# Cumulative log decays summed once in the projections and read back per chunk, in a chunkwise hybrid recurrence

## The chip, the cores and the metric

The kernel runs on one core of one Trainium2 chip. The metric is the device time of one execution in microseconds (us). All tensors are float32; matmuls whose operands are of type fp32r take one pass over their columns, those of plain float32 operands several, and the trace shows each of the latter as two records.

## What is computed

One layer of a hybrid encoder trunk on 2048 tokens of width 1024: an RMSNorm, one wide input projection, three token mixers, gates, an output projection and a final norm. The change touches the third mixer, a gated DeltaNet in chunkwise form (8 value heads, 4 key heads of 128). Cut to what matters:

```python
log_a = -jnp.exp(a_log) * softplus(c_a + dt_bias)      # one number per token and head
g = jnp.cumsum(log_a, axis=-1)                          # within a chunk
diff = g[..., :, None] - g[..., None, :]
decay_causal = masked_exp(diff, causal)
m = einsum('tk,sk->ts', k, kb) * decay_strict           # kb = k * beta
sol = triangular_solve(I + m, [v, k * exp(g)])
a_qk = einsum('tk,sk->ts', q, kb) * decay_causal
q_inter = q * exp(g);  k_state = kb * exp(g_last - g)
# per chunk: e = u - w S;  o = q_inter S + a_qk e;  S = exp(g_last) S + k_state^T e
```

The kernel uses chunks of 128 tokens (it calls them windows, 16 of them), which gives the same result as the 64 of the reference. The second mixer, HGRN2, runs beside it in the same windows, with its own decays in seven levels.

## The kernel before

Four blocks follow one another, each with its own instruction lists for PE, ACT, DVE, POOL and the DMA-issuing SP, tied by semaphores: `norm_and_transpose` (to about 80 us), `project` (to about 1625 us), `recur` (to about 2275 us) and `merge`. Each engine runs its list in the order in which it is written, so the order of work is the order of the calls in these lists.

`project` makes 80 pairs of output tiles, with seven block products each of 12 fp32r matmuls of 512 columns. `decays_begun` and `decays_ended` (L1229, L1236) leave the log decays and betas of all 2048 tokens in `keep["ab"]`. `fill_masks` (L110) writes the masks on POOL after its last operand.

`recur` works on windows w, with v = w + 1 prepared while w is finished. What the change and the prediction speak of:

- Log decays. `log_decays` (L1486) spreads one window's log decays over a causal mask on POOL, in a high and a low fp32r part (`la_t`). `decays_between` on PE (L1592) multiplies them with `later_r` into the banks `M[0]`, `M[1]`, which gives g_t - g_s in every place, and `decays_from_start` (L1599) with `ones_r` into `M[2]`, `M[3]`, which gives g_t. ACT turns the first into `dec` (L1868) and the second into `eg` (L1874). POOL multiplies `dec` with the betas (`weighted_decays`, L1499), DVE multiplies the products of keys with keys and queries by it (`an_keys` L2054, `an_queries` L2059), and POOL makes the decayed queries from `eg` (L1519).
- Triangular inverse. `blocks_out` (L1416) sends `ak` to DRAM and reads its 16x16 diagonal blocks back as `X`; DVE inverts them (`substitute`); `inverses_back` (L1423) brings them into `T` and `R`. PE and DVE then double the inverse three times: `level_w` and `level_z` with l = 4, 5, 6 on PE (L1692, L1712; L1692, L1709; L1690, L1706), `level_32`, `level_64` and `level_128` on DVE (L2126 to L2144).
- HGRN2. `scores(w, l)` on PE (L1663 to L1669) reads `kql`, which DVE makes in `pair_kq` (L2093) and `level_kq` (L2108).
- End of a window. `products_e`, `products_o`, `products_ds` (L1720 to L1749), the norms of the outputs, and `norms(v + 1)` on PE (L1585), which ACT reads in `key_norms` (L1858, L1860) before `hx_inv` (L1882), the operand of DVE's next `pair_kq`.

The PE list of a window (L1804 on) is: `turn_v`, `products_ks`, `level_w` 4, `turn_k`, `turn_hv`, `decays_between(v)`, `level_z` 4, `products_kq(v)`, `scores` 0, `decays_from_start(v)`, `level_w` 5, `scores` 1, `level_z` 5, `scores` 2, `level_w` 6, `scores` 3, `level_z` 6, `scores` 4, `products_e` and the rest. In windows 1 to 14 the two decay calls stand in this list; those for v = 0 and 1 stand ahead of the loop.

## Time and profile before

| | us |
|---|---|
| median of 3 runs | 2839.93 |
| lowest, highest | 2833.96, 2846.58 |
| the profiled execution | 2831.88 |
| its span, first to last instruction | 2830.1 |
| mean granted TensorE clock | 0.984 of full |
| busy: PE, DVE, ACT, POOL | 2731.2, 1848.6, 1239.0, 1473.3 |

The profile gives for each engine the time in which an instruction of it ran, and for TensorE also the clock that was granted (1.00 is 2.4 GHz, 0.50 is 1.2 GHz). A timeline row has its start, its length (of all instructions merged in it), engine, line, output and inputs, and in brackets how long the engine was idle before it and who ended that.

### The profile page before, as it was taken

Reading aid. Unit: us, or ns where it says so; the run is one execution under the profiler, and the core shown is the slowest. Engines: PE = TensorE matmul, PEld = TensorE weight load, DVE = VectorE, ACT = ScalarE, POOL = GpSimd, SP = SyncE. Lnnn points to the kernel's source line nnn. Section 1 sums busy time; section 2 is a strip of 40 time slices with the busy share of each in tenths; the row PEclk is TensorE's granted clock in tenths of the full one; section 3 lists DMA queues with packets and bytes.
Section 4 is the critical chain, followed back from the end, with each engine's and each line's share of the span. In section 5 each row is a group of like instructions: output and inputs, shape, how many; then the busy total and the mean of one; then the engine's idle time right before and its main releaser. Section 6 shows DMA issues by size and latency. Waiting matters only on the chain. (4 is left out here: it accounts for less than half of the span.)

```text
span 2830.1 us, 39377 instructions
## 1 busy us (share of the span) xinstructions
PE 2731.2 (97%) x14135; PEld 2286.3 (81%) x14135; DVE 1848.6 (65%) x2902; ACT 1239.0 (44%) x2153; POOL 1473.3 (52%) x1135
## 2 busy tenths in 40 slices
PE   7999999999998999999999979999999979999999
PEld 5788888888877888888888768888888867888877
DVE  7777777773248788878722258888888765445453
ACT  7443444444453444444444435566555543222221
POOL 0554555554446555555554466666777435453441
PEclk9999999999999999999999979999999989999999
DMA  6333333334463333333343356665555557555552
GB/s 188 97 112 104 91 112 104 99 95 120 111 183 94 112 90 105 108 106 92 104 119 97 107 129 155 155 154 132 130 134 149 136 180 234 162 182 172 171 174 76
DMA packets 536937, 366.05 MB, mean 129 GB/s; under 512 B 65462, under 2 KB 469032, under 8 KB 536744
## 3 DMA queue, kind: packets, MB, share of 16 engines
q1 hardware_dynamic: 536744, 363.52, 45.2%
q8 instruction: 115, 1.88, 0.3%
q14 instruction: 78, 0.64, 0.1%
HBM read 251.27 MB, written 112.20 MB: 128 GB/s over the span
## 5 line engine op out<-in xcount | busy, mean ns | idle before, releaser
L767 POOL TENSOR_TENSOR w_low<-w_raw,w_high 128x512 fp32r<-128x512 f32 x479 | 684.9, 1435 | 634.8 <-ACT w_high L846 634.7
L800 PE MATMUL p_x<-h_high,w_high 128*128 128x512 f32 x1280 | 500.3, 391 | 13.1 <-ACT u L975 6.5
L800 PE MATMUL p_x<-h_low,w_high 128*128 128x512 f32 x1280 | 499.3, 390 | 0.0
L800 PE MATMUL p_x<-h_high,w_low 128*128 128x512 f32 x1280 | 499.2, 390 | 0.0
L846 ACT ACTIVATE w_high<-w_raw 128x512 fp32r<-128x512 f32 x479 | 296.5, 627 | 246.8 <-PE p_z L800 141.3
L800 PEld LDWEIGHTS p_x<-h_high,w_high 128*128 128x128 f32 x1280 | 240.8, 188 | 66.2 <-ACT u L975 7.3
L800 PEld LDWEIGHTS p_x<-h_low,w_high 128*128 128x128 f32 x1280 | 240.9, 188 | 50.2
L800 PEld LDWEIGHTS p_x<-h_high,w_low 128*128 128x128 f32 x1280 | 241.0, 188 | 49.8
L800 PE MATMUL p_z<-h_high,w_high 128*128 128x512 f32 x640 | 249.2, 389 | 0.0
L800 PE MATMUL p_z<-h_low,w_high 128*128 128x512 f32 x640 | 249.1, 389 | 0.0
L800 PE MATMUL p_z<-h_high,w_low 128*128 128x512 f32 x640 | 249.1, 389 | 0.0
L2442 PE MATMUL b_o<-m_yh,m_wo_high 128*128 128x512 f32 x512 | 202.0, 394 | 21.9 <-DVE m_yl_lead L2578 12.5
L2403 POOL TENSOR_TENSOR m_wo_low<-m_wo_raw_lead,m_wo_high 128x512 fp32r<-128x512 f32 x86 | 118.8, 1384 | 180.4 <-ACT m_wo_high L2497 180.3
L1098 DVE TENSOR_TENSOR c_raw<-p_z,u 128x512 f32<-128x512 f32 x72 | 49.8, 691 | 241.6 <-PE p_x L800 181.3
L2442 PE MATMUL b_o<-m_yh,m_wo_low 128*128 128x512 f32 x512 | 201.0, 393 | 0.0
L767 POOL TENSOR_TENSOR w_low<-w_s,w_high 128x512 fp32r<-128x512 f32 x80 | 114.8, 1435 | 97.9 <-ACT w_high L846 97.3
L1510 POOL TENSOR_TENSOR dx<-hin 128x256 f32<-128x256 f32 x112 | 76.4, 682 | 132.4 <-ACT hx L1893 118.4
L1114 DVE SCALAR_TENSOR_TENSOR ring<-c_raw,cols,ring 128x512 f32<-128x512 f32 x128 | 142.3, 1112 | 4.5
L2541 DVE TENSOR_TENSOR w_raw<-b_o,ring 128x512 f32<-128x512 f32 x96 | 65.8, 690 | 121.2 <-PE b_o L2442 97.0
L800 PEld LDWEIGHTS p_z<-h_high,w_high 128*128 128x128 f32 x640 | 120.2, 188 | 25.2 <-DVE c_raw L1098 0.2
L800 PEld LDWEIGHTS p_z<-h_low,w_high 128*128 128x128 f32 x640 | 120.1, 188 | 25.0
L800 PEld LDWEIGHTS p_z<-h_high,w_low 128*128 128x128 f32 x640 | 120.1, 188 | 24.9
(300 smaller groups left out, 6096.6 us busy)
## 6 DMA issues: line engine op xcount, KB each, us to landing
w_raw<-in_w_in_dram SPq DMA_DIRECT2D x160, 512.0 KB, 5.2
branch_scratch<-ring SPq DMA_DIRECT2D x176, 256.0 KB, 5.2
gate_scratch<-ring SPq DMA_DIRECT2D x96, 256.0 KB, 6.0
ring<-gate_scratch SPq DMA_DIRECT2D x96, 256.0 KB, 4.0
hin<-branch_scratch SPq DMA_DIRECT2D x16, 1280.0 KB, 11.6
zin<-branch_scratch SPq DMA_DIRECT2D x16, 1024.0 KB, 7.0
m_wo_raw_lead<-in_w_out_c_dram SPq DMA_DIRECT2D x43, 256.0 KB, 3.1
xin<-in_x_dram SPq DMA_DIRECT2D x16, 512.0 KB, 3.9
```

The costliest lines, as they stand in the source:

```text
L767: nc.gpsimd.tensor_tensor(wl(j), place(p, j), wh(j).bitcast(F32), ALU.subtract).then_inc(low, 1)
L800: x = nc.tensor.matmul(to[:], w(j)[:, k, :], h[:, j, k, :], start=(opens and k == 0 and a == 0), stop=(k == HK - 1 and a == 2), skip_group ...
L846: fn(wh(j), place(p, j), ACT.Copy).then_inc(high, 1)
L1098: tt(of_unit(p, 1, 1), Z[p % 2][:], u3[:], ALU.add).then_inc(c22, 1)
L1114: link(stt(out, src, w, out, ALU.mult, ALU.add))
L1510: tt(free_ap(dx[:, l % 2, :], 0, halves), left, mid, ALU.subtract)
L2403: tt(wl[:, u % SLOTS, :, :], wraw(u), raw(wh[:, u % SLOTS, :, :]), ALU.subtract).then_inc(w_low, 1)
L2442: x = nc.tensor.matmul(bank, w[:, u % SLOTS, k, :], y(4 * i + k), start=(i < 3 and k == 0 and a == 0), stop=(i != 2 and k == 3 and a == 2))
L2541: tt(to, bank, gt[:, b, :], ALU.mult).then_inc(gated, 1)
```

## The change

The sums g of the log decays are formed once, in `project`. At pair 8 PE multiplies the log decays of all windows with four 128x128 masks (causal, after, ones, and a causal mask less its middle column, "centred"); ACT copies the four results out, PE transposes two of them (sums from the start and centred sums) so that a window's head is a row, ACT copies these too, and SP stores both forms in DRAM. The causal mask is filled at pair 3 instead of at the end, and DVE makes the other two at pair 6.

In `recur` SP loads, for each window, one row of 1024 numbers into all 128 partitions, once of the centred sums (`rows_centred`) and once of the sums from the start (`rows_start`). POOL subtracts the centred sum of the row's own token (`col[:, 3, v, :]`) and cuts the difference at 0 (`exponents`), in place of `log_decays`; ACT takes exponentials of these in place, and of `rows_start` in one instruction. PE's `decays_between` and `decays_from_start` are gone, with the waits that kept their banks apart. Both loads stand behind `blocks_out` in SP's list.

```diff
@@ project: SP @@
+                    if p == 12:
+                        sp.wait_ge(rows_kept, 1)
+                        sp.dma_start(front["decay_rows"].rearrange("i r n -> r i n"), kept_rows).then_inc(decays_out, 16)
+                        sp.dma_start(front["decay_sums"], t3_flat[:, 0:4 * P]).then_inc(decays_out, 16)
@@ project: PE @@
+                def decay_sums_of():
+                    pe.wait_ge(causal_cut, 1)
+                    pe.wait_ge(sum_masks, 2)
+                    for i, which in enumerate((causal[:], after, keep["ones"][:], centred)):
+                        x = nc.tensor.matmul(sums_bank[:, i, :], which, ab[:, :, 0:dm.vh], start=True, stop=True)
+                    x.then_inc(decay_sums, 1)
+                def decay_rows_of():
+                    pe.wait_ge(sums_kept, 1)
+                    for i, at in enumerate((0, 3)):
+                        x = nc.tensor.transpose(rows_bank[:, i, :], kept_sums[:, at, :], keep["ident"][:])
...
@@ project: ACT @@
+                    if p == 9:
+                        act.wait_ge(decay_sums, 1)
+                        fn(kept_sums, sums_bank[:], ACT.Copy).then_inc(sums_kept, 1)
+                    if p == 11:
+                        act.wait_ge(decay_rows, 1)
+                        fn(kept_rows, rows_bank[:, 0:2, :], ACT.Copy).then_inc(rows_kept, 1)
@@ recur: SP @@
+                def load_centred(v):
+                    wait(sp, v - 1, "diff_ready", 1)
+                    sp.dma_start(rows_centred[:].rearrange("p h n -> p (h n)"), bass.AP(rows.tensor, (win + v) * V * P, [[0, P], [1, V * P]])
+                                 ).then_inc(centred_in, 16)
+                def load_start(v):
+                    wait(sp, v - 1, "eg_ready", 1)
...
+                sp.dma_start(col[:].rearrange("p i w c -> p (i w c)"), front["decay_sums"]).then_inc(col_in, 16)
+                load_centred(0)
+                load_start(0)
                 load(0)
...
                 load_k(1)
+                load_centred(1)
+                load_start(1)
                 blocks_out(0)
                 load(1)
                 inverses_back(0)
+                load_centred(2)
...
                         blocks_out(w + 1)
+                        if w + 2 < win:
+                            load_start(w + 2)
+                        if w + 3 < win:
+                            load_centred(w + 3)
                         inverses_back(w + 1)
@@ recur: POOL @@
-                def log_decays(v):
-                    wait(pool, v - 1, "m_ga", 2)
-                    for i in range(2):
-                        tt(la_t[:, i, :, :], free_ap(masks["causal"][:], 0, [[0, V], [1, P]]), spread(la_parts[:, i, v, :].bitcast(F32), P),
-                           ALU.mult).then_inc(sems["la_ready"], 1)
+                def exponents(v):
+                    pool.wait_ge(centred_in, 16 * v + 16)
...
+                    wait(pool, v - 1, "aq_ready", 2)
+                    tt(dec[:], rows_centred[:], spread(col[:, 3, v, :], P), ALU.subtract).then_inc(sems["diff_ready"], 1)
+                    wait(pool, v, "diff_ready", 1)
+                    nc.gpsimd.tensor_scalar(dec[:], dec[:], 0.0, None, ALU.min).then_inc(sems["diff_ready"], 1)
@@ recur: PE, in the loop @@
-                    if 0 < w < win - 1:
-                        decays_between(v)
                     level_z(w, 4)
...
-                    if 0 < w < win - 1:
-                        decays_from_start(v)
                     level_w(w, 5)
@@ recur: ACT @@
+                    wait(act, v, "diff_ready", 2)
                     for g in range(2):
-                        wait(act, v, "m_gb", g + 1)
-                        fn(four(dec, g), M[g][:], ACT.Exp).then_inc(sems["dec_ready"], 1)
+                        fn(four(dec, g), four(dec, g), ACT.Exp).then_inc(sems["dec_ready"], 1)
...
-                    for g in range(2):
-                        wait(act, v, "m_ga", g + 1)
-                        fn(four(eg, g), M[2 + g][:], ACT.Exp).then_inc(sems["eg_ready"], 1)
+                    act.wait_ge(start_in, 16 * v + 16)
+                    fn(eg[:], rows_start[:], ACT.Exp).then_inc(sems["eg_ready"], 1)
```

DVE's list inside the loop is the same in both kernels. On PE, from `level_w` 4 to `products_e` of a window, the list was this (`b_m`, `b_g`, `b_h` are the banks M, G and HB):

```order
L1692 MATMUL b_g<-T,ak 128x64 x8
L1639 MATMUL b_m<-ident,qkn 128x128 x4
L1645 MATMUL b_m<-ident,hin 128x128 x4
L1589 MATMUL b_m<-la_t,later_r 128x512 x4
L1712 MATMUL b_g<-W,R 128x64 x8
L1612 MATMUL b_m<-qkn 128x256 x4
L1663 MATMUL b_h<-kql 128x128 x4
L1589 MATMUL b_m<-la_t,ones_r 128x512 x4
L1692 MATMUL b_g<-T,ak 128x64 x8
L1669 MATMUL b_h<-kql 128x64 x4
L1709 MATMUL b_g<-R,W 64x64 x8
```

In the changed kernel the same stretch reads:

```order
L1732 MATMUL b_g<-T,ak 128x64 x8
L1679 MATMUL b_m<-ident,qkn 128x128 x4
L1685 MATMUL b_m<-ident,hin 128x128 x4
L1752 MATMUL b_g<-W,R 128x64 x8
L1654 MATMUL b_m<-qkn 128x256 x4
L1703 MATMUL b_h<-kql 128x128 x4
L1732 MATMUL b_g<-T,ak 128x64 x8
L1709 MATMUL b_h<-kql 128x64 x4
L1749 MATMUL b_g<-R,W 64x64 x8
```

The two groups of four 512-column matmuls are gone and nothing stands in their place. SP's list in a window of the changed kernel, from the store of the outputs to the inverse blocks, is:

```order
L1467 DMA y_scratch<-ring 128x8x128
L1471 DMA an_scratch<-ak 128x8x128
L1474 DMA X<-an_scratch 64x16x16
L1447 DMA rows_start<-decay_rows_scratch 128x1024
L1442 DMA rows_centred<-decay_rows_scratch 128x1024
L1483 DMA inverse_scratch<-XI 64x16x16
L1485 DMA inverse_scratch<-XT 64x16x16
```

The two loads of 128x1024 are new; the instructions around them are those of before, in their order.

## Rows read from the trace of the kernel before

**Rows 1.** The page, busy time of each engine.

```profile
PE 2731.2 (97%) x14135; PEld 2286.3 (81%) x14135; DVE 1848.6 (65%) x2902; ACT 1239.0 (44%) x2153; POOL 1473.3 (52%) x1135
```

**Rows 2.** Stretches: length, busy PE, PEld, DVE, ACT, POOL, clock, DMA share, GB/s.

```profile
1780.20:1817.90 37.70, 37.07 (x297) 32.91 (x295) 31.87 (x91) 22.57 (x44) 26.70 (x24) 1.00 0.58 145
...
1912.00:1922.00 10.00, 9.36 (x93) 8.82 (x91) 9.18 (x34) 4.14 (x8) 10.00 (x10) 1.00 0.08 8
```

**Rows 3.** Timeline of PE, from one window's `norms` to the next one's.

```profile
1893.49 1.88 PE L1585 MATMUL b_m<-w_raw,ones 128*128 128x512 f32 x4
...
1901.20 1.21 PE L1589 MATMUL b_m<-la_t,later_r 128*128 128x512 f32 x4
1902.24 1.89 PE L1712 MATMUL b_g<-W,R 128*128 128x64 f32 x16
...
1906.57 1.17 PE L1589 MATMUL b_m<-la_t,ones_r 128*128 128x512 f32 x4
1907.57 1.89 PE L1692 MATMUL b_g<-T,ak 128*128 128x64 f32 x16
...
1913.68 0.68 PE L1690 MATMUL b_g<-T,ak 128*64 128x64 f32 x8 [0.60 <-DVE T L2139]
...
1931.18 1.02 PE L1585 MATMUL b_m<-w_raw,ones 128*128 128x512 f32 x2
```

**Rows 4.** Timeline of ACT in that window, from `key_norms` to `hx_inv`.

```profile
1894.62 0.69 ACT L1858 ACTIVATE rn<-b_m,eps 128x512 f32<-128x512 f32 x1 [0.54 <-PE b_m L1585]
...
1897.11 0.61 ACT L1882 ACTIVATE hx_inv<-dx 128x512 f32<-128x512 f32 x1
```

**Rows 5.** Timeline of DVE in that window.

```profile
1897.85 0.69 DVE L2093 TENSOR_TENSOR kql<-hin,hx_inv 128x512 f32<-128x512 f32 x1 [2.24 <-ACT hx_inv L1882]
...
1906.92 1.13 DVE L2108 TENSOR_TENSOR kql<-hin,hx 128x512 f32<-128x512 f32 x1
...
1913.31 0.31 DVE L2139 STREAM_TRANSPOSE T<-b_g 32x128 f32<-32x128 f32 x1
```

**Rows 6.** Waits of PE, 1700 to 2235 us: who, total, times, longest.

```profile
PE b_g L1690 <- DVE T L2139: 8.4, 14, 0.6
PE b_g L1720 <- DVE R L2144: 1.2, 3, 0.6
```

**Rows 7.** Three windows' `products_e` on PE, a stretch, and two of DVE's window starts.

```profile
1765.03 3.64 PE L1720 MATMUL b_g<-w_raw,R 128*128 128x128 f32 x16 [0.61 <-DVE R L2144]
...
1955.61 2.05 PE L1720 MATMUL b_g<-w_raw,R 128*128 128x128 f32 x16 [0.32 <-DVE R L2144]
...
1993.83 3.68 PE L1720 MATMUL b_g<-w_raw,R 128*128 128x128 f32 x16 [0.31 <-DVE R L2144]
...
1994.00:1997.20 3.20, 3.20 (x16) 3.20 (x17) 2.75 (x10) 0.62 (x2) 3.20 (x3) 0.50 0.01 3
...
1744.64 0.69 DVE L2093 TENSOR_TENSOR kql<-hin,hx_inv 128x512 f32<-128x512 f32 x1 [2.31 <-ACT hx_inv L1882]
...
1784.79 0.69 DVE L2093 TENSOR_TENSOR kql<-hin,hx_inv 128x512 f32<-128x512 f32 x1 [2.23 <-ACT hx_inv L1882]
```

**Rows 8.** Window 0: two stretches, and two rows of PE's timeline.

```profile
1670.00:1674.00 4.00, 4.00 (x21) 4.00 (x20) 1.14 (x2) 0.38 (x1) 0.00 (x0) 0.50 0.00 0
...
1690.00:1694.00 4.00, 4.00 (x39) 3.88 (x38) 2.29 (x10) 1.38 (x3) 3.00 (x5) 0.99 0.02 6
...
1657.78 2.06 PE L1589 MATMUL b_m<-la_t,ones_r 128*128 128x512 f32 x4
...
1685.96 1.97 PE L1669 MATMUL b_h<-kql 128*128 128x64 f32 x8
```

**Rows 9.** Two groups of POOL instructions, and a load with its KB and time to landing.

```profile
L1489 POOL TENSOR_TENSOR la_t<-causal,la_parts 128x1024 fp32r<-128x1024 f32 x32 | 60.1, 1898 | 7.2 <-DVE la_parts L2189 7.2
L1499 POOL TENSOR_TENSOR dec<-dec,db 128x1024 f32<-128x1024 f32 x16 | 38.0, 2377 | 50.5 <-ACT dec L1868 50.5
...
w_raw<-in_final_norm_w_dram SPq DMA_DIRECT2D x1, 512.0 KB, 5.7
```

More of the change, by code:

```diff
@@ L597, in project @@
         X, Y, Z = ([bank(f"p_{n}{i}") for i in range(2)] for n in "xyz")
+        sums_bank, rows_bank = (c.enter_context(nc.psum_tensor(f"p_sums{i}", [P, 4, P], F32)) for i in range(2))
+        causal = keep["masks"]["causal"]
+        ab = keep["ab"][:, 0:dm.win * 2 * dm.vh].rearrange("p (w c) -> p w c", c=2 * dm.vh)
         own_sems = []
@@ L632, in project @@
         t2 = craw[:, 0, :, 3:3 + 2 * BLK]
+        t3_flat = t3[:].rearrange("p a n -> p (a n)")
+        kept_sums, kept_rows = (t3_flat[:, at:at + n * P].rearrange("p (i n) -> p i n", n=P) for at, n in ((0, 4), (4 * P, 2)))
+        centred, after = t3_flat[:, 6 * P:7 * P], t3_flat[:, 7 * P:8 * P]
         form_place = {P1: wide(work[:]), P5: wide(work[:]), P2: wide(lows_of(P5)), P6: t2, P4: wide(ring[:]), P3: wide(lows_of(P3))}
@@ L1256, in _ @@
                         decays_ended()
+                    if p == 6:
+                        dve.wait_ge(causal_cut, 1)
+                        tt(centred, causal[:], spread(causal[:, P // 2 - 1:P // 2], P), ALU.subtract).then_inc(sum_masks, 1)
+                        tt(after, keep["ones"][:], causal[:], ALU.subtract).then_inc(sum_masks, 1)
                     q, more = before(p), p + 1 < N
@@ L1571, in _ @@
                 mm, turn, ident = nc.tensor.matmul, nc.tensor.transpose, keep["ident"][:]
-                def columns():
-                    for i, which in enumerate((masks["causal"][:], later_r[:].bitcast(F32), keep["ones"][:])):
-                        x = mm(G[0][:, i, :], which, ab[:, :, 0:V], start=True, stop=True)
-                    x.then_inc(m_col, 1)
                 def norms(v):
@@ L1585, in norms @@
                         mm(M[g][:], keep["ones"][:], sq[:, g, :], start=True, stop=True).then_inc(sems["m_ssq"], 1)
-                def sum_parts(bank, which, g):
-                    for i in range(2):
-                        x = mm(bank[:], which[:], four(la_t[:, i, :, :], g), start=(i == 0), stop=(i == 1))
-                    return x
-                def decays_between(v):
-                    wait(pe, v, "la_ready", 2)
-                    wait(pe, v, "rn_ready", 3)
-                    for g in range(2):
-                        wait(pe, v - 1, "res", 4 * g + 4)
-                        sum_parts(M[g], later_r, g).then_inc(sems["m_gb"], 1)
-                def decays_from_start(v):
-                    if v > 0:
-                        wait(pe, v - 1, "hv_ready", 1)
-                        wait(pe, v - 1, "kt_ready", 1)
-                    for g in range(2):
-                        sum_parts(M[2 + g], ones_r, g).then_inc(sems["m_ga"], 1)
                 def products_kq(v):
@@ L1885, in level_exp @@
                     elif l == 2:
-                        wait(act, w + 1, "eg_ready", 2) if more else wait(act, w, "kt_ready", 1)
+                        wait(act, w, "kt_ready", 1)
                     elif l == 3:
@@ L1889, in level_exp @@
                     elif l == 4:
-                        wait(act, w + 1, "eg_ready", 1) if more else wait(act, w, "hv_ready", 1)
+                        wait(act, w, "hv_ready", 1)
                     else:
```

88 lines of the change are left out of this document (42 added, 46 removed).

## The prediction

> **What bounds the kernel now.** I read the page first, then the stretches of one window of `recur`, the timelines of PE, ACT and DVE in it, the waits, and last the clock. The page shows PE busy for 97% of the span [rows 1], so every matmul taken away looks like time won. In a window of `recur` PE is busy for 37.07 of 37.70 us, DVE for 31.87 and POOL for 26.70 [rows 2]. But a busy engine need not be the one that sets the pace. The timelines show a loop through three engines. PE's `norms` start at 1893.49 [rows 3]; ACT waits for them, starts at 1894.62 and ends with `hx_inv` at 1897.11 [rows 4]; DVE waits for that and starts at 1897.85 [rows 5]. From there to the last transpose of `T` at 1913.31 it has no idle time at all. PE waits 0.60 us for this transpose, starts again at 1913.68, and then runs without a gap to the next `norms` at 1931.18, which is 37.69 us after the first. The wait for DVE is no accident of one window: it stands in all 14, 8.4 us in all, never over 0.6 [rows 6]. So from 1897.85 to 1913.31 DVE sets the pace, and PE, although busy, runs beside it with 0.6 us to spare.
>
> **What the change takes away on PE.** The two groups of decay matmuls last 1902.24 - 1901.20 = 1.04 us and 1907.57 - 1906.57 = 1.00 us, start to next start [rows 3]: 2.04 us in each of 14 windows, 28.6 us. Both lie in the part that DVE paces, and DVE's own list there is unchanged. So I count their removal at nothing: PE comes to the wait for `T` 2.04 us earlier, and waits there and at the places just before it. Where these new waits lie can be worked out. `scores` 1 needs the `kql` that DVE has ready at 1906.92 + 1.13 = 1908.05 [rows 5], while PE, 2.04 us ahead, would be done with `level_w` 5 at about 1907.4. It waits some 0.7 us there, some more at `scores` 2 and `level_w` 6, and again before the second half of that: 2.6 us in all instead of 0.6, spread over the 64-column matmuls.
>
> **What that does to the clock.** The granted clock is at 1.00 (2.4 GHz) in nearly all of the windows. Twice it fell to 0.50 (1.2 GHz), each time just as `products_e` began, after the stretch of 64-column matmuls; `products_e` then took 3.64 and 3.68 us instead of 2.05, and the stretch reads 0.50 [rows 7]. What was different in these two windows? In three windows of the fourteen PE had a second wait, for `R` at L1720, of 0.61, 0.32 and 0.31 us [rows 6, 7]. Two of the three are the two falls; the eleven windows without it have none. So a few tenths of a microsecond more of waiting in this stretch were enough. The change puts 2.0 us more into it, in every window, and takes out the densest work next to it. I therefore expect the clock to fall in most of the windows.
>
> How long does it stay down? In window 0 the clock read 0.50 while PE ran the same `level_w`, `level_z` and `scores`, busy for 4.00 of 4.00 us, and it came back at 1690, after `products_e` had started [rows 8]. So I expect it to stay down until the 128-column products. The price at 0.50: `scores` takes 1.97 us there [rows 8], and 1.1 would be the pace of half that and a little, so each of the seven calls from `scores` 1 to `scores` 4 costs about 0.87 more, 6.1 in all, and `products_e` 3.64 - 2.05 = 1.6 more [rows 7]. Of this sum of 7.7, the 2.6 us in which PE would have waited anyway cost nothing: 5.1 us a window if the fall comes at the first wait. The lower end is a fall at `products_e` alone. The window with the 0.61 us wait lasted 1784.79 - 1744.64 = 40.15 us [rows 7], 2.46 over the 37.69, and 1.85 without that wait. I take 3.4, about the middle, since where in the stretch it falls should vary from window to window: 14 x 3.4 = 47.6 us more, and less the two falls that the profiled execution has already paid, 2 x 2.5 = 5 us. The ends are 14 x 1.85 = 26 and 14 x 5.1 = 71 us.
>
> The Trainium skill has two rules that bear on this, both in "TensorE: Matmul & The Clock Gate". The section "HAM oscillation — how this bites in real kernels" makes the loss of the clock a matter of long gaps between matmuls. By it gaps of well under a microsecond would do nothing, and the time would be the first rival's. The stretch at 0.50 with PE busy throughout [rows 8] speaks against it. The section "A second HAM failure mode: psum-queue depth-cycling" says that short idles, if frequent, make the clock swing between its two levels, which is what the two falls look like, and by it the change is a loss.
>
> **The other parts.** POOL: two products of 1.90 us [rows 9] give way to a subtraction of the same shape, with one spread operand (1.90, from the same row), and a minimum with a constant, of which the trace has no row. It lies between nothing and the 2.38 us of a product of two full operands [rows 9]; I take 1.9, the row nearest in what it reads. That gives -1.9 to +0.5 us on POOL, which has 11 us free in a window [rows 2]. Its `differences` for levels 5 to 7 stand behind it, and ACT's exponentials for them wait a few tenths already; half a microsecond more is hidden by `blocks_in`, which comes ahead of them on ACT. ACT reads the same number of elements as before, and no longer waits for PE's sums, in a part where nothing waits for it: nothing. SP: two loads of 512 KB more a window. The only row of such a load, one line into all partitions, is the final norm's weights, 5.7 us to landing [rows 9]. They are issued behind the blocks of `X`, when the DMA share is 0.08 for 10 us [rows 2], and their data is used a window later: nothing. If each took twice as long they would run into the inverse blocks, which reach PE with a few microseconds to spare. SP's waits ahead of them (for `eg` and for the subtraction) end before the inverse is ready, so that nothing queued behind is late.
>
> `project`: PE, which bounds it, gets four products of 128 plain float32 columns and two transposes. `norms` does two of 512 columns in 1.88 us [rows 3], so 0.24 us for 128: six times that is 1.4 us. The two copies on ACT, the mask on POOL and the two on DVE lie where these engines wait for PE: nothing, and if this cover were gone, some 2 us once.
>
> Start of `recur`: three loads now stand ahead of the operands and two more ahead of `ak`, 2.25 MB or four and a half times the load that takes 5.7 us alone [rows 9]; several are in flight at a time, and I put the first `X` 4 to 8 us later. Against this the decay matmuls of windows 0 and 1 go, 2.06 us for one group at half clock [rows 8], three such on the path, and with them the wait of ACT. Bounds -6 to +6; I take +1.
>
> **Sum**, against the profiled execution of 2831.9: + 47.6 - 5 + 1.4 + 1 = **2877 us**. That execution is 8.0 us below the median of the three, 2839.9. I add nothing for this: falls of the clock in other windows would explain the difference, and they are in the sum already.
>
> **Rivals.**
> 1. *Nothing happens.* The waits grow, but the clock holds as before. For it: one of the three windows with the second wait kept its clock, and 2.6 us are 7% of a window. Time: 2831.9 + 2.4 = 2834. Chance 0.16.
> 2. *Short falls only.* The clock falls in each window, but only as `products_e` begins, as in the two seen: + 26 - 5 + 2.4, 2855 us. Chance 0.14, half of it within 0.5%.
> 3. *The matmuls were on the path.* The saving is real if DVE itself runs ahead once PE does: several of DVE's instructions read banks that PE fills only a tenth before (`T`'s and the ones of `scores`), and idle time of that size would not show. Then the windows shrink by the full 2.04 us: 2831.9 - 28.6 + 2.4 = 2806 us. It decides as soon as DVE's 15.5 us from `kql` to `T` become shorter, which its own instruction lengths, adding up to the whole of it, speak against. Chance 0.12.
> 4. The forecast, 0.58.
>
> **Numbers.** What a measurement of this kernel can tell from no change is about 0.5%, here 14 us: faster is below 2825.7, slower above 2854.1. Slower: 0.58 and half of rival 2, 0.65. Same: the other half and rival 1, 0.23. Faster: 0.12. The range reaches from 2826, which leaves out rival 3, to 2905, near the upper end of the cost of the falls (2831.9 + 71 - 5 + 2.4 = 2900) with some of the start's; what is left out is under 0.2. The forecast's own range is 2855 to 2905.
>
> **What would show it.** In the profile after: PE idle before `scores` 1, `scores` 2 and `level_w` 6, ended by DVE, over 2 us a window; DVE's stretch from `kql` to the last transpose of `T` still about 15.5 us where the clock is at 1.00; the clock at 0.50 in ten or more windows, from somewhere in the 64-column stretch into `products_e`; windows of 40 to 42 us. The forecast is wrong if the mean clock in `recur` stays at 0.98 or more, or if windows at full clock are well below 37.7 us, and its size is wrong if the falls are there but end at once.

## The result, and the profile after

| | before | after |
|---|---|---|
| median of 11 runs each | 2830.6 us (2819.5 to 2846.6) | 2867.6 us (2850.5 to 2880.9) |
| after / before | | 1.0119, 95% interval 1.0096 to 1.0142 |
| profiled execution (span) | 2831.9 (2830.1) | 2864.1 (2862.4) |
| clock, mean over the span | 0.984 | 0.968 |

The change makes the kernel 1.2% slower. The forecast was 2877, with a range of 2826 to 2905: the sign is right, the value 9 us high. It was a rise of 45 us over the profiled execution of before; the medians differ by 37 us, the two profiled executions by 32.2. Every "before" in the table of the experiments below was measured again beside the runs that it is compared with. The ratios leave out two executions at a lower clock, one of e3 (3437.4 us, mean clock 0.746) and one of before beside e1 to e4 (2859.5 us).

The profiled executions differ by 32.2 us. The starts of DVE's first `kql` in each window (L2116, before L2093) divide this:

| stretch | before | after | difference |
|---|---|---|---|
| to the first memset of `recur` | 1626.9 | 1630.0 | +3.1 |
| from there to the start of window 1 | 80.1 | 87.9 | +7.8 |
| windows 1 to 14 | 531.0 | 553.3 | +22.3 |
| the rest | | | -1.0 |

The page's row for the engines answers to [rows 1]:

```profile
PE 2743.8 (96%) x14011; PEld 2299.3 (80%) x14011; DVE 1840.1 (64%) x2900; ACT 1235.4 (43%) x2139; POOL 1489.0 (52%) x1135
```

PE has 124 matmuls fewer and is busy for 12.6 us more. That alone says that its matmuls have become longer: work was taken away, and time did not go with it. Three stretches of the changed kernel (columns as in [rows 2]) show both kinds of window:

```profile
1717.90:1755.68 37.78, 35.73 (x288) 31.66 (x287) 31.51 (x91) 22.34 (x43) 27.60 (x24) 1.00 0.65 172
...
1870.60:1912.30 41.70, 40.15 (x288) 36.09 (x287) 31.92 (x91) 22.29 (x43) 27.66 (x24) 0.88 0.61 157
...
1885.80:1896.00 10.20, 10.12 (x56) 9.77 (x57) 6.78 (x23) 3.08 (x6) 10.20 (x10) 0.50 0.37 107
```

The first is window 1 at full clock, the second window 5, and the third the 10.2 us of window 5 with the clock at 0.50 (1.2 GHz). The two windows have the same 288 matmuls. PE is busy 35.7 us in the one and 40.2 in the other. In the third stretch it is busy for 10.12 of 10.20 us, as in window 0 in [rows 8]: a busy PE is no sign of a fast one.

PE's waits in windows 1 to 14, which answer to [rows 6]:

```profile
PE b_g L1730 <- DVE T L2162: 17.9, 28, 0.7
PE b_h L1709 <- DVE kql L2131: 3.5, 16, 0.4
PE b_g L1760 <- DVE R L2167: 2.0, 4, 0.7
```

Where there was one wait for `T` in a window there are two, of 0.64 us each, and a new one of 0.21 us before `scores` 2. PE's timeline of window 2 shows their places:

```profile
1763.51 1.90 PE L1732 MATMUL b_g<-T,ak 128*128 128x64 f32 x16
1765.48 1.11 PE L1709 MATMUL b_h<-kql 128*128 128x64 f32 x8
1766.51 1.15 PE L1749 MATMUL b_g<-R,W 128*64 128x64 f32 x16
1767.87 1.10 PE L1709 MATMUL b_h<-kql 128*128 128x64 f32 x8 [0.21 <-DVE kql L2131]
1769.62 0.68 PE L1730 MATMUL b_g<-T,ak 128*64 128x64 f32 x8 [0.65 <-DVE T L2162]
1770.93 0.68 PE L1730 MATMUL b_g<-T,ak 128*64 128x64 f32 x8 [0.63 <-DVE T L2162]
```

And the same places in window 5, where the clock falls at 1885.8, at the end of the second wait:

```profile
1884.58 0.68 PE L1730 MATMUL b_g<-T,ak 128*64 128x64 f32 x8 [0.65 <-DVE T L2162]
1885.88 1.11 PE L1730 MATMUL b_g<-T,ak 128*64 128x64 f32 x8 [0.63 <-DVE T L2162]
1886.93 1.97 PE L1709 MATMUL b_h<-kql 128*128 128x64 f32 x8
1888.83 1.97 PE L1746 MATMUL b_g<-R,W 64*64 64x64 f32 x16
1890.73 1.97 PE L1709 MATMUL b_h<-kql 128*128 128x64 f32 x8
1892.48 3.70 PE L1760 MATMUL b_g<-w_raw,R 128*128 128x128 f32 x16
1896.01 1.02 PE L1709 MATMUL b_h<-kql 128*128 128x64 f32 x8
```

Each `scores` takes 1.97 us there instead of 1.10, and `products_e` 3.70 instead of 2.05. The full pace is back at 1896.0. Such falls stand in nine of windows 1 to 14 (3, 5, 6, 7 and 10 to 14). They last 3.4 us in window 3 and 6.8 or 10.2 us in the others. Before there were two, of 3.4 us each.

Not foreseen is what DVE did. Its stretch from `kql` to the last transpose of `T`, 15.46 us in [rows 5], is 14.90 us now:

```profile
1717.90 0.69 DVE L2116 TENSOR_TENSOR kql<-hin,hx_inv 128x512 f32<-128x512 f32 x1 [2.31 <-ACT hx_inv L1905]
...
1725.58 1.25 DVE L2077 TENSOR_TENSOR ak<-b_m,dec 128x512 f32<-128x512 f32 x2
1726.75 0.90 DVE L2131 TENSOR_TENSOR kql<-hin,hx 128x512 f32<-128x512 f32 x1
1727.58 0.68 DVE L2123 TENSOR_TENSOR A<-b_h,pairs 128x512 f32<-128x512 f32 x1
...
1732.80 0.31 DVE L2162 STREAM_TRANSPOSE T<-b_g 32x128 f32<-32x128 f32 x1
```

From the first `kql` to `A` are 9.68 us here, and 1907.97 - 1897.85 = 10.12 before. Where the 0.56 us of the whole stretch went can be read from the starts. `ak` starts 0.14 us earlier and the `kql` behind it 0.22; `A` is 0.44 ahead and the next step on `A` (L2118, now L2141) 0.55. The last 0.1 lies at this step, which before started 0.11 us after PE's `scores` 1 (1909.30 + 1.06). Most of the rest comes over POOL, whose rows before and after are:

```profile
1903.27 2.37 POOL L1499 TENSOR_TENSOR dec<-dec,db 128x1024 f32<-128x1024 f32 x1 [3.12 <-ACT dec L1868]
1905.61 1.89 POOL L1524 TENSOR_TENSOR ks<-kt,col 128x1024 f32<-128x1024 f32 x1
```

```profile
1722.87 2.38 POOL L1566 TENSOR_TENSOR dec<-dec,db 128x1024 f32<-128x1024 f32 x1 [2.67 <-ACT dec L1892]
1725.20 1.90 POOL L1591 TENSOR_TENSOR ks<-kt,col 128x1024 f32<-128x1024 f32 x1
```

POOL's weighted decays `dec` wait for ACT's exponentials, which before waited for PE's sums. They ended 7.79 us after the window's first `kql`, and DVE's `ak` started 0.03 us behind; now they end at 7.35, and `ak` starts 0.33 later, as soon as DVE is free. And the `kql` of level 1, "1.13 us" long in [rows 5] and 0.90 now, is not held by PE. It starts while POOL's `ks` is running and ends 0.55 us after that product, in each of windows 1 to 14 of both kernels. In e1, where `ks` is over before it starts, it takes 0.77. So DVE had been held up, by POOL and by PE, in pieces so small that the rows gave them to the instructions. That PE's list is behind it, e1 shows: with nothing but matmuls put back on PE the stretch is 15.95 us. The period of a window at full clock went from 37.69 to 37.12 us.

With this the 22.3 us of windows 1 to 14 can be put together from the periods:

- the period at full clock: 14 x -0.57 = -8.0;
- the nine windows with a fall, over 37.12 (over 34.80, the length in e2, for the last, which is shorter): 2.97 + 4.52 + 3.40 + 4.41 + 3.21 + 4.56 + 3.22 + 4.51 + 3.21 = +34.0, which is 3.8 each;
- the late `X` in three windows without a fall (1, 2 and 9): +1.9;
- the two falls and a few late `X` of before: -5.6.

The sum is +22.3, as in the table.

### The profile page after: what moved, and what is told of

It is laid out like the page before. It is cut to its first block and busy times, and to the rows that moved or that the text cites. A ratio compares the mean times of both kernels' runs of the same rounds, so it can differ in the third digit from the quotient of the medians.

```text
span 2862.4 us, 39166 instructions
## 1 busy us (share of the span) xinstructions
PE 2743.8 (96%) x14011; PEld 2299.3 (80%) x14011; DVE 1840.1 (64%) x2900; ACT 1235.4 (43%) x2139; POOL 1489.0 (52%) x1135
```

## The experiments

All variants but one start from the changed kernel. The filler in them is a matmul of 128x512 on constant ones, whose result nobody reads. The table counts PE's waits for DVE's `kql`, `T` and `R` (to 2260 us) and the falls of the clock in windows 1 to 14 of the profiled execution.

| kernel | PE waits for DVE, us | windows with a fall | median, us | ratio to before, 95% |
|---|---|---|---|---|
| before | 10.2 | 2 | 2830.6 | |
| after | 23.4 | 9 | 2867.6 | 1.0119 (1.0096 to 1.0142) |
| e1 filler in the old places | 8.6 | 0 | 2842.8 | 1.0036 (1.0011 to 1.0061) |
| e2 filler in the waits | 8.7 | 1 | 2838.5 | 1.0019 (0.9993 to 1.0045) |
| e3 before, half the sums | 15.0 | 2 | 2832.0 | 0.9996 (0.9967 to 1.0025) |
| e4 rows loaded once | 22.1 | 10 | 2870.2 | 1.0137 (1.0068 to 1.0205) |
| e5 one filler, before `scores` 1 | 24.6 | 5 | 2866.5 | 1.0127 (1.0084 to 1.0169) |
| e6 = e2, `hin` behind `X` | 5.0 | 1 | 2831.9 | 1.0004 (0.9987 to 1.0021) |
| e7 = e2, first loads reordered | 8.4 | 1 | 2836.2 | 1.0018 (0.9997 to 1.0040) |
| e8 = e2, minimum twice | 17.1 | 9 | 2873.4 | 1.0138 (1.0102 to 1.0174) |
| e9 = e6, minimum at the end | 7.4 | 2 | 2832.6 | 1.0006 (0.9986 to 1.0027) |
| e10 = e9 and first loads | 6.2 | 1 | 2831.0 | 1.0001 (0.9979 to 1.0023) |
| e11 = e10, no filler | 21.5 | 10 | 2873.8 | 1.0141 (1.0108 to 1.0175) |
| e12 = e10, POOL's order at the start | 7.8 | 1 | 2828.3 | 0.9991 (0.9973 to 1.0009) |

### e1: as much work for PE as before, in the same places

```diff
+                def fill(banks, n):
+                    for b in banks:
+                        for i in range(n):
+                            mm(b[:], ones_r[:], free_ap(ones_r[:], 0, [[0, 4], [1, P]]), start=(i == 0), stop=(i == n - 1))
                         turn_hv(w)
+                    if 0 < w < win - 1:
+                        fill_between(v)
                     level_z(w, 4)
...
                         scores(w, 0)
+                    if 0 < w < win - 1:
+                        fill_start(v)
                     level_w(w, 5)
```

`fill_between` puts two fillers into each of `M[0]` and `M[1]`, `fill_start` four into `HB[1]`.

> The changed kernel with matmuls put back on PE that compute nothing used: four of 128x512 in the place of the sums between tokens (before level_z 4) and four after scores 0, as dense as the decay matmuls that the change removed. Loads, POOL's and ACT's new work are as in the change. If the clock falls because PE has less to do and waits in small pieces: two or fewer falls in windows 1 to 14 instead of nine, the stretch from kql to the last transpose of T back at 15.4 to 15.5 us, windows of 37.7, and a time of 2838 to 2845 (before's 2830.6 and the 11 us lost ahead of window 1). If the loads, the wait for X or POOL's minimum make the windows longer: falls stay near nine and the time stays at 2865 or more, since PE has more to do.

Measured: 2842.8 us and no fall in windows 1 to 14. The filler takes 1.01 us in each place, as the sums did [rows 3], and PE waits once in a window again:

```profile
1758.22 1.17 PE L1826 MATMUL b_m<-ones_r 128*128 128x512 f32 x4 [0.28 <-issue]
1759.23 1.89 PE L1753 MATMUL b_g<-W,R 128*128 128x64 f32 x16
...
1770.65 0.68 PE L1731 MATMUL b_g<-T,ak 128*64 128x64 f32 x8 [0.59 <-DVE T L2182]
```

The windows are 38.17 us, not 37.7, since the filler brings a start of its own of 0.28 us and a wait for both halves of `res` at once. The stretch from `kql` to `T` is 15.95 us, above the 15.4 to 15.5 expected. But this kernel does everything that the change added (the loads, POOL's subtraction and minimum, ACT's exponentials) and 2 us of useless work a window on top, and is 25 us faster than the changed kernel. So neither the loads nor POOL's new work made it slow by themselves.

### e2: work for PE only where it stands still

```diff
                     level_w(w, 5)
+                    if 0 < w < win - 1:
+                        wait(pe, w - 1, "y_h", 1)
+                        fill(HB[1:2], 1)
                     if w > 0:
                         scores(w, 1)
...
                         scores(w, 2)
+                    if 0 < w < win - 1:
+                        wait(pe, w, "h_pred", 2)
+                        fill(HB[1:2], 2)
                     level_w(w, 6)
...
+                            if g == 1 and 0 < w < win - 1:
+                                fill(HB[1:2], 2)
                             wait(pe, w, "t_half", 2 * g + 2)
```

> The changed kernel with the same kind of 128x512 matmul (0.26 us each at full clock) only where PE now waits for DVE: one before scores 1 (wait 0.21), two before level_w 6 (0.66) and two between its halves (0.63). They take time in which PE stood still. If waits of a few tenths are what brings the clock down: no more than two falls, windows at 37.1 to 37.7, kql to T still 14.9, and 2834 to 2842, at least as fast as the filler in the old places. If it is the amount of work that PE lost over the whole window (2 us) and not these waits: 1.3 us of filler is too little, falls stay at five or more, time 2850 or more. If it is the loads or POOL: no change, 2865.

Measured: 2838.5 us, one fall. PE's timeline of window 2, beside that of the changed kernel above:

```profile
1763.94 0.48 PE L1828 MATMUL b_h<-ones_r 128*128 128x512 f32 x1
1764.26 1.05 PE L1710 MATMUL b_h<-kql 128*128 128x64 f32 x8
...
1766.59 1.10 PE L1710 MATMUL b_h<-kql 128*128 128x64 f32 x8 [0.21 <-DVE kql L2157]
1767.51 0.71 PE L1828 MATMUL b_h<-ones_r 128*128 128x512 f32 x2
1768.35 0.68 PE L1733 MATMUL b_g<-T,ak 128*64 128x64 f32 x8
1768.95 0.73 PE L1828 MATMUL b_h<-ones_r 128*128 128x512 f32 x2
1769.65 0.68 PE L1733 MATMUL b_g<-T,ak 128*64 128x64 f32 x8
```

The halves of `level_w` 6 start where they would have started anyway, and windows without a fall are 37.11 us: the filler costs nothing. One point of the expectation was wrong. The wait of 0.21 us stands before `scores` 2 and is still there. The first filler lies before `scores` 1, where the trace shows no wait, though PE had some to spare: the filler takes 0.32 us there and delays `scores` 1, counted from the start of `level_w` 5, by 0.06 (2.03 instead of 1.97). That leaves the four at `level_w` 6, about 1 us in all, as the ones that fill a wait of any size; e5 looks at this.

### e3: less work for PE in the kernel before

```diff
                 def sum_parts(bank, which, g):
-                    for i in range(2):
-                        x = mm(bank[:], which[:], four(la_t[:, i, :, :], g), start=(i == 0), stop=(i == 1))
+                    for i in range(1):
+                        x = mm(bank[:], which[:], four(la_t[:, i, :, :], g), start=True, stop=True)
                     return x
```

> The kernel before with only the first of the two matmuls of every decay sum (the high part of the log decays, the low part is left out of the sums), so PE has 1.0 us less to do in each of windows 1 to 14; no new load, nothing changed on POOL, ACT or DVE. If the clock reacts to PE's missing work and its waits: falls in four or more of windows 1 to 14 instead of two, kql to T shorter by some tenths, and a time of 2838 to 2855. If the loads or POOL's new work bring the falls of the changed kernel: two or three falls as before and 2826 to 2832.

Measured: 2832.0 us, no different from before. This fell between the expectations. Half of the mechanism is there, with nothing changed but PE's work: the windows became 37.32 us instead of 37.69, `kql` to `T` 15.10 instead of 15.46 (`ak` is no longer held, while the `kql` of level 1 still takes 1.09 us beside POOL's `ks`), and PE's waits for `T` doubled in number:

```profile
PE b_g L1690 <- DVE T L2139: 12.8, 29, 0.6
PE b_g L1720 <- DVE R L2144: 2.2, 4, 0.7
```

But falls did not become more frequent: windows 6 and 10, a third in window 15. They are longer, 6.8 us instead of 3.4, so that their windows took 40.5 us. Shorter windows at full clock (14 x -0.37 = -5.2 us), dearer falls (+1.8) and more of the other delays, in six windows of 0.2 to 1.1 us each (+2.8), nearly cancel. One microsecond less for PE is not enough to bring the clock down in most windows; two are.

### e4: the loads taken away

```diff
                 def load_centred(v):
+                    if v > 2:
+                        return
                     wait(sp, v - 1, "diff_ready", 1)
...
                 def load_start(v):
+                    if v > 1:
+                        return
```

and the two waits for these loads go up to these windows only.

> The changed kernel in which the spread rows are loaded only for windows 0 and 1 (the centred ones also for 2) and used again in all later windows, so that the decays of windows from 2 or 3 on are another chunk's. PE, POOL, ACT and DVE do the same instructions. If the 1 MB a window is hidden: nine falls more or less, time within 5 us of the changed kernel's 2867.6; the waits for X may go, worth at most their 7.6 us. If contention of these loads is what costs: windows back at 37.1 and 2840 or less.

Measured: 2870.2 us in four runs (1.0068 to 1.0205), ten falls, no different from the changed kernel. Without the loads the DMA engines move less (135 instead of 163 GB/s on average), and DVE's waits for `X` are 5.3 us instead of 7.6. That is all that 1 MB a window costs there: about 2 us.

### e5: one filler only

```diff
                     level_w(w, 5)
+                    if 0 < w < win - 1:
+                        wait(pe, w - 1, "y_h", 1)
+                        fill(HB[1:2], 1)
                     if w > 0:
                         scores(w, 1)
```

> The changed kernel with one filler matmul of 128x512 before scores 1 alone. The two waits of 0.66 and 0.63 us at level_w 6 stay. If the falls come from those two waits, or from the little work in that part of the window: five or more of windows 1 to 14 still have a fall and the time is 2852 to 2868. If it is enough that PE has something to do once more in each window: two falls or fewer, 2845 or less.

Measured: 2866.5 us in the median. The profiled execution, with a span of 2845.5, was the fastest of its runs, and has falls in five windows (2, 3, 5, 8 and 9). The two waits for `T` are as in the changed kernel:

```profile
PE b_g L1731 <- DVE T L2183: 17.9, 28, 0.7
PE b_h L1710 <- DVE kql L2152: 4.1, 16, 0.7
```

So one more matmul does not do it; by the difference to e2, it takes the four at `level_w` 6. Whether these four alone are enough was not tried. The median is 19 us above the profiled execution, so five falls are probably fewer than a typical run of e5 has.

### e6: `hin` behind `X`

In the changed kernel, and still in e2, DVE waits for `X` in nine windows. `ak` goes out to DRAM behind 2.3 MB of operands for the next window. Here the larger part of these, `hin`, is issued later.

```diff
                 def load(w):
...
-                    sp.dma_start(hin[:, w % 2, :, :], s_dram[0:NH, :, cut(w)].rearrange("t p n -> p t n")).then_inc(h_in[w % 2], 16)
+                    if w < 2:
+                        load_h(w)
...
                         blocks_out(w + 1)
+                        if w >= 1:
+                            load_h(w + 1)
```

> The kernel with filler in the waits, and the load of hin for the next window (1280 KB) issued behind the load of X instead of ahead of ak's way out. If X comes late because ak's 512 KB stand behind 2.3 MB of operands in the queues: DVE's waits for X, 8.7 us in nine windows, fall under 2 us, windows are 37.1 to 37.4 and the time is 5 to 8 us below that kernel's 2838.5. If X's way is limited by its own small pieces: no change in the waits. Against it: hin might come late to POOL's first differences or stand in the way of the inverse blocks; then level_w 4 waits for T or R, and it is slower by 1 us or more a window.

Measured: 2831.9 us, 6.6 below e2. DVE's waits for `X` in windows 1 to 14 are, in e2 and here:

```profile
DVE X L2112 <- DMA X<-an_scratch: 8.7, 9, 1.5
```

```profile
DVE X L2118 <- DMA X<-an_scratch: 2.1, 2, 1.5
```

Ten of windows 1 to 13 are 37.11 to 37.15 us; two have a late `X` (37.66 and 37.83), one the fall (41.08). Neither `hin` nor the inverse blocks came late. In e9, e10 and e12, which have the same order, the waits for `X` were 4 to 7 us, so that part of this gain does not last from run to run.

### e7: the first loads in another order

```diff
+                load_centred(0)
+                load(0)
+                load_k(1)
+                load_start(0)
+                blocks_out(0)
+                load_centred(1)
+                sp.wait_ge(zeroed, 1)
+                for d in inv_dram:
+                    sp.dma_start(whole(d), S[:]).then_inc(zero_out, 16)
+                load_start(1)
+                load(1)
+                inverses_back(0)
```

> The kernel with filler in the waits, and another order of the first loads of recur: the spread rows of window 1, the zeroes for the inverse blocks and the start rows of window 1 go behind ak and X of window 0. Ahead of ak's landing stand 4.3 MB instead of 5.8. If the late first X (1656.9 in the changed kernel, 1645.2 before) is a matter of that queue: X 5 to 9 us earlier, and the time 4 to 8 us below 2838.5. If the clock at 0.50 in window 0 sets its length: X earlier, but the start of window 1 moves less than 3 us.

Measured: 2836.2 us, and a start of `recur` that is as long as before it: window 1 begins 88.2 us after the first memset, as with 87.9 in the changed kernel, though `X` came 5.6 us earlier (21.3 us after the memset instead of 26.9). The first theory failed. The number of the second fits, but its reason is not all of it: another chain, which e10 makes visible, took the place of `X`, and the clock in window 0 has a part too, as e11 and e12 show.

### e8: the minimum twice

```diff
                     nc.gpsimd.tensor_scalar(dec[:], dec[:], 0.0, None, ALU.min).then_inc(sems["diff_ready"], 1)
+                    wait(pool, v, "diff_ready", 2)
+                    nc.gpsimd.tensor_scalar(dec[:], dec[:], 0.0, None, ALU.min).then_inc(sems["diff_ready"], 1)
```

> The kernel with filler in the waits, and POOL's minimum with 0 done twice (2.8 us more POOL work a window). If POOL has the room that its 29 of 37 busy microseconds suggest: within 4 us of 2838.5. If the exponentials of levels 5 to 7 behind the differences set the pace (ACT waits 0.4 to 0.55 us for POOL at each of them): 1 to 2.8 us a window more, 2853 to 2878, and then the first minimum has already cost something in the changed kernel.

Measured: 2873.4 us. The shortest windows are 39.69 us instead of 37.11: 2.58 us for an instruction of 2.77. The wait shows on ACT:

```profile
ACT b_m L1944 <- POOL dx L1581: 48.8, 26, 4.0
```

In e2 this row reads 13.8 us. POOL is busy for 27.6 of 37.1 us in e2 and yet has only 0.2 us of room ahead of the `differences` of level 5. The rest of its idle time lies in one piece, behind `differences` 0, where it waits up to 8.8 us for ACT. The first minimum, 2.77 us where I had taken 1.9, has therefore used up the room to almost nothing, and cost nothing. There is a second lesson here: with the filler as in e2, nine windows have a fall of 3.4 us. New waits at other places (PE waits 12.8 us for `kql` and 7.7 for `e`) bring the clock down too.

### e9: the minimum where POOL waits

The minimum becomes a function of its own, `clip`, which POOL does behind `differences(v, 0)` at the end of its window.

```diff
                     if v < win:
                         differences(v, 0)
+                    if v + 1 < win:
+                        clip(v + 1)
```

> The kernel with filler in the waits and hin behind X (2831.9), and POOL's minimum moved from ahead of the differences of levels 5 to 7 to the end of POOL's window, where POOL otherwise waits up to 8.8 us for ACT. If the minimum cost nothing where it stood (a second one there cost 2.6 of its 2.8 us, so the first left only 0.2 us of room): windows stay at 37.11 and the time within 2 us of 2831.9. If ACT's waits for POOL's differences had been holding back kql of levels 5 and 6 and with them the late matmuls: windows under 37.0 and up to 5 us less. At the end of the window it stands ahead of nothing that is awaited; if it does, 1 us a window more.

Measured: 2832.6 us, windows at 37.11 to 37.13: no difference, as the 0.2 us of room said. It stays in the versions below.

### e10 and e11: all together, and without filler

e10 is e9 with the first loads as in e7 and `load(1)` behind `inverses_back(0)`. e11 is e10 without `fill`.

> The kernel of e9, and the first loads reordered as in e7, now with the second operand load (2.3 MB) behind the inverse blocks of window 0 too. In e7 X came 5 us earlier and window 1 did not, since the zeroes and 2.3 MB stood ahead of the inverse blocks. If that queue was the reason: window 1 starts 4 to 7 us earlier (80 to 84 us after the first memset of recur instead of 87.5), and the time is 2824 to 2829, faster than before by 0.1 to 0.2%. If not: as e9.

> The kernel of e10 without any filler matmul. If the falls of the clock come from PE's short waits for DVE: six or more of windows 1 to 14 have one, as in the changed kernel, and it is 20 to 30 us slower than e10, at 2845 to 2858. If the late X or POOL's minimum had helped to bring them about: three or fewer, and within 8 us of e10.

Measured: e10 2831.0 us, e11 2873.8. The two differ by the five filler matmuls a window alone, and they divide one fall from ten, and 43 us. e11's PE waits are those of the changed kernel:

```profile
PE b_g L1742 <- DVE T L2174: 17.9, 28, 0.7
PE b_h L1721 <- DVE kql L2143: 2.9, 14, 0.2
```

43 us is more than the 20 to 30 that I expected, and more than the 32.9 us between the two profiled spans (2827.6 and 2860.5; in windows 1 to 14 alone 522.7 and 558.4, since e11 got to window 1 4.5 us sooner). How many falls a run has varies, and a profile shows one run.

The start of e10 missed its expectation: window 1 again 88.3 us after the memset. POOL's rows say why:

```profile
1645.59 0.61 POOL L1586 TENSOR_TENSOR dx<-hin 128x256 f32<-128x256 f32 x1
1646.16 0.61 POOL L1587 TENSOR_TENSOR dx<-hin 128x256 f32<-128x256 f32 x1
1652.22 1.90 POOL L1562 TENSOR_TENSOR dec<-rows_centred,col 128x1024 f32<-128x1024 f32 x1 [5.45 <-DMA rows_centred<-decay_rows_scratch]
1654.20 2.77 POOL L1566 TENSOR_SCALAR dec<-dec 128x1024 f32<-128x1024 f32 x1
1656.94 1.90 POOL L1570 TENSOR_TENSOR db<-causal,neg_b 128x1024 f32<-128x1024 f32 x1
1658.79 2.34 POOL L1595 TENSOR_TENSOR qg<-qkn,eg 128x1024 f32<-128x1024 f32 x1
```

The decayed queries `qg` of window 0 stand behind a wait for the rows of window 1 and 6.6 us of work for window 1. DVE's `keys(1)` may overwrite `qkn` only behind `qg`: it starts at 1661.32.

But this chain is not all that sets the start. e11 has the same order and the same work up to there, its second `X`, that of window 1, comes at the same time (62.8 us after the memset, 62.9 in e10), and yet its window 1 begins at 83.7 us instead of 88.3. What differs is the clock: it is back at 1.00 61.6 us after the memset in e11, and 71.9 in e10.

### e12: POOL's order at the start

```diff
-                exponents(1)
-                clip(1)
-                betas(1)
                 pool.wait_ge(cols, 2)
...
                     differences(w, 2)
+                    if w == 0:
+                        exponents(1)
+                        clip(1)
+                        betas(1)
```

> The kernel of e10 in which POOL forms the exponents and weights of window 1 behind the first decayed queries and the differences of level 2, instead of ahead of them. In e10 X came 5 us earlier than in the changed kernel, but POOL waited 5.5 us for the rows of window 1 and then did 6.6 us of work for it, and the decayed queries of window 0 stood behind: DVE's keys of window 1 waited for them until 1661.3. If this chain sets the start: window 1 begins 83 to 85.5 us after the first memset of recur instead of 88.3, and the time is 2826 to 2829. If PE at half clock sets it: less than 1.5 us earlier, and as e10.

Measured: window 1 begins 84.1 us after the memset, 4.2 earlier than in e10. The gain is there at the `X` of window 1, which comes 58.8 us after the memset instead of 62.9, and from there to window 1 both kernels take 25.3 to 25.4 us. `qg` is done before the wait:

```profile
1649.69 2.35 POOL L1595 TENSOR_TENSOR qg<-qkn,eg 128x1024 f32<-128x1024 f32 x1
...
1654.44 1.90 POOL L1562 TENSOR_TENSOR dec<-rows_centred,col 128x1024 f32<-128x1024 f32 x1 [0.25 <-DMA rows_centred<-decay_rows_scratch]
```

The time is 2828.3 us against 2830.5 for before beside it, 0.9991 (0.9973 to 1.0009). That is the best version found. It is 1.3% faster than the change as it came (1.0119 / 0.9991), and it can't be told from the kernel before.

## Why the prediction was right, and where it was not

**DVE sets the pace, so PE's 2.04 us are worth nothing.** Nearly right. Of the 2.04 us, 0.57 were a gain, in a period of 37.12 instead of 37.69 us. The step that failed is that DVE's own instruction lengths add up to the whole of its stretch, which I took as proof that nothing held it up. The lengths, and gaps too short to be shown, contained waits: some 0.45 us over POOL, whose `dec` and `ks` stood behind PE's sums, and 0.1 for `scores` 1. Rival 3 had named just this, "idle time of that size would not show", and holds for a quarter of its saving, -8.0 us; but the banks that it names as the way explain only the 0.1.

**The waits move to three places.** Right in kind: before `scores` 2 and before both halves of `level_w` 6. Before `scores` 1, where 0.7 us were forecast, no row shows a wait, but from the start of `level_w` 5 to it are 1.97 us where there were 1.73, so 0.24 us were lost. The waits shown are 0.21 + 0.65 + 0.63 = 1.5 us in most windows and not 2.6. The rest is the 0.57 us by which the window is shorter, and about half a microsecond in pieces that no row of waits shows (PE is idle for 37.78 - 35.73 = 2.05 us in window 1).

**The clock falls.** Right, and shown: the filler in PE's waits (e2, and e10 against e11) leaves the other engines' work as it is and takes falls from nine or ten windows to one. Taking the loads away (e4) or moving the minimum and the loads with no filler (e11) leaves them where they were.

The size came out of two errors that cancel in part. Falls came in nine windows in the profiled execution, where the forecast counted fourteen. Each cost 3.8 us, not 3.4, over a window at full clock. 14 x 3.4 = 47.6 became 34.0. The length explains the price. Four falls begin in the second half of `level_w` 6, about 15 us into the window, and last 10.2 us; four begin near 18 us, behind `level_z` 6, and last 6.8; all go on into `products_e`. So these eight are the forecast's case, though none begins as early as `scores` 1, and only the one in window 3, of 3.4 us, is that of rival 2. Rival 1, the same change with its clock held, is what e2 and e10 are: 2838.5 and 2831.0 us where it said 2834.

Of the two sections of the Trainium skill's page "TensorE: Matmul & The Clock Gate", the runs agree with "A second HAM failure mode: psum-queue depth-cycling", by which frequent short idles make the clock swing: here PE waits of 0.2 to 0.66 us, and filling them brought 28 to 43 us back. The section "HAM oscillation — how this bites in real kernels" of the Trainium skill's page "TensorE: Matmul & The Clock Gate" speaks of long gaps, and what it says does not cover these falls: no wait of PE in these windows is longer than 0.7 us.

**POOL.** The minimum took 2.77 us, outside the bounds of 0 to 2.38. The step that failed is the price by the nearest row: an instruction with one operand and a constant is slower here than one with two. It is hidden all the same, but by 0.2 us (e8), and not by the 11 us that the forecast named as its room, most of which lies elsewhere in the window.

**SP and the loads.** They land in 4.5 and 5.0 us, where 5.7 was taken, and cost some 2 us in all through `X` (e4). Taken: nothing.

**`project`.** Comparing the 559 high parts that ACT forms there, one by one, the changed kernel is 2.3 us late before the sums are reached, 3.5 behind them and 3.8 from about 900 us on. So the sums cost 1.2 and later parts 0.3, together 1.5 where 1.4 was taken. The 2.3 us are no part of the change: e2, e4, e7 and e12 have them too and e1, e5, e6, e9 and e10, with the same code up to there, do not; and e3, whose `project` is that of before, is 2.4 us late as well. The 0.3 may be no part of it either, as e3 loses 1.1 us more in the same place.

**Start of `recur`.** Mis-sized: +1 was taken, with bounds of -6 and +6, and it measured +7.8. The delay of `X` was nearly right (4 to 8 us were taken; it is 26.88 - 18.34 = 8.5). What failed is the credit against it, some 6 us for the decay matmuls of windows 0 and 1, of which the start shows nothing. No run took this apart, but the clock is a likely place for it. In window 0 it stood at 0.50 for 47.7 us instead of 34.1. In e4, whose code is that of the change up to there but for two loads that are not repeated, it was 37.5 us, and window 1 began 85.0 us after the memset instead of 87.9. So some 3 us of the 7.8 probably come and go with it. And the cause is not `X` alone. In e7 and e10 `X` came 5 us sooner and window 1 did not; POOL's wait for the rows was the next chain, and e12, which puts `qg` ahead of it, gains 4.1 us by the `X` of window 1.

The sum in the forecast's terms: 34.0 + 1.9 (falls and late `X`) - 5.6 (those of before) - 8.0 (the shorter period) + 1.5 (`project`) + 7.8 (start) = +31.6, and 2.3 - 0.7 for the early lag and a shift of the first memset on DVE, -1.0 for the rest: 32.2, as measured.

Open: whether the chip reacts to PE's idle time or to the work that is missing in that stretch. In e1 and e2 both were changed back together. e8 speaks for idle time, since it has all the work of e2 and nine falls. But e3 has 15.0 us of waits and no more falls than before with 10.2. And e5 has as many waits as the change and five falls where that has nine, though this is e5's fastest execution, and by its median a typical one has more. Which window falls in which run is not explained by anything that I read.

## What to carry to other kernels

Work taken off an engine that waits for another one is no gain, and on PE it can be a loss: before removing matmuls, look at what stands between them, and whether the short waits that take their place lie in a stretch of small matmuls. A few dense matmuls that compute nothing, placed exactly in those waits, cost nothing and here gave back 28 us (e2 against the change, by their ratios) to 43 (e10 against e11). And ask of an engine's idle time where it lies: POOL had nearly 10 us in each window and 0.2 us at the place that mattered.

## What the runs showed of the hardware

- The clock fell to 0.50 with no wait of PE longer than 0.7 us, from some 2 us of idle time in a window of 37. While it was down, PE was busy for 10.12 of 10.20 us, and the low clock lasted 3.4, 6.8 or 10.2 us.
- POOL, 128x1024 float32: the subtraction with one spread operand takes 1.90 us, the product of two full operands 2.38, the minimum with a constant 2.77. The one that reads least is the slowest.

```profile
L1557 POOL TENSOR_SCALAR dec<-dec 128x1024 f32<-128x1024 f32 x13 | 36.0, 2766 | 1.1
L1566 POOL TENSOR_TENSOR dec<-dec,db 128x1024 f32<-128x1024 f32 x13 | 30.9, 2379 | 34.7 <-ACT dec L1892 34.7
...
L1555 POOL TENSOR_TENSOR dec<-rows_centred,col 128x1024 f32<-128x1024 f32 x13 | 24.7, 1898 | 0.0
```

- A DVE product of two operands in SBUF that starts while a POOL instruction runs is shown as longer, not as idle. The `kql` of level 1 takes 1.10 to 1.16 us before, 0.88 to 0.91 after and 0.77 in e1, and ends each time 0.55 us after the POOL instruction that ran at its start; the first `kql` of a window, with POOL idle, takes 0.69. POOL's next instruction is longer for it too (`dx` 1.06 us instead of 0.61).
- In window 0, behind 5.8 MB of transfers issued ahead of it, the 512 KB of `ak` took from 1646.1 to about 1653.5 us to land, against 4.3 to 5.2 us in windows 2 to 6.
